# Earlier loads for three phases, and keys turned in place, in a one-core hybrid decoder step

## The reference, cut to what matters

```
logits = jnp.einsum('bqhe,bqkhe->bqhk', qg, kg) * SCALE
p, lse = masked_softmax(logits + bias[None], valid[None, :, None, :])
o = jnp.einsum('bqhk,bqkhe->bqhe', p.astype(vg.dtype), vg)
```

```
ha = jnp.einsum('bcjge,jef->bcgf', ch, w1[:CMP_STRIDE])
hb = jnp.einsum('bcjge,jef->bcgf', ch, w1[CMP_STRIDE:])
h = jax.nn.gelu(ha[:, :-1] + hb[:, 1:] + const)
```

## Time and profile before

| what | value |
|---|---|
| median of 3 runs | 2420.94 us (2412.12 to 2422.14) |
| the profiled execution | 2420.17 us, span 2418.3 us |
| mean granted TensorE clock | 0.914 |
| PE busy | 2060.2 us (85%) |
| DVE busy | 1248.5 us (52%) |
| ACT busy | 889.8 us (37%) |
| POOL busy | 141.9 us (6%) |
| DMA | 341.78 MB, mean 141 GB/s |

### The profile page before, as it was taken

The page is one execution under the profiler, slowest core; times in us unless marked ns, Lnnn a source line. Parts: engine busy times, 40 slices in busy tenths (PEclk is TensorE's granted clock), DMA queues, the critical chain, the costliest instruction groups (busy, mean ns, idle before and its releaser), DMA issues. The chain is left out here.

```text
span 2418.3 us, 40665 instructions
## 1 busy us (share of the span) xinstructions
PE 2060.2 (85%) x15344; PEld 1719.2 (71%) x15344; DVE 1248.5 (52%) x2596; ACT 889.8 (37%) x1482; POOL 141.9 (6%) x428
## 2 busy tenths in 40 slices
PE   7996567565987999999979679669997889999997
PEld 5993245443566999988779545446675779999786
DVE  4224456876754555544532468524444645555445
ACT  2211233234722544533221167523343234454432
POOL 3001000100000111100000000000000001111000
PEclk9997788787998999999989589879999889999999
DMA  5356288533132556642123331273331235665421
GB/s 164 127 189 203 80 315 288 206 150 121 50 122 95 194 201 217 205 146 74 61 95 84 107 94 47 75 215 146 119 131 39 93 117 200 218 203 191 140 82 49
DMA packets 169184, 341.78 MB, mean 141 GB/s; under 512 B 38175, under 2 KB 106319, under 8 KB 165051
## 3 DMA queue, kind: packets, MB, share of 16 engines
q1 hardware_dynamic: 152638, 200.40, 26.2%
q10 hardware_dynamic: 12956, 85.06, 10.5%
q0 software_dynamic: 3456, 54.53, 5.7%
HBM read 312.91 MB, written 97.35 MB: 170 GB/s over the span
## 5 line engine op out<-in xcount | busy, mean ns | idle before, releaser
L235 PE MATMUL ffn_acc<-x_h,ffn_wh 128*128 128x288 f32 x1408 | 303.5, 297 | 11.3 <-DVE ffn_wl L227 11.3
L235 PE MATMUL ffn_acc<-x_l,ffn_wh 128*128 128x288 f32 x1408 | 303.0, 297 | 0.0
L235 PE MATMUL ffn_acc<-x_h,ffn_wl 128*128 128x288 f32 x1408 | 302.8, 297 | 0.0
L235 PEld LDWEIGHTS ffn_acc<-x_h,ffn_wh 128*128 128x128 f32 x1408 | 228.2, 190 | 11.8 <-DVE ffn_wl L227 11.7
L235 PEld LDWEIGHTS ffn_acc<-x_l,ffn_wh 128*128 128x128 f32 x1408 | 228.3, 190 | 0.0
L235 PEld LDWEIGHTS ffn_acc<-x_h,ffn_wl 128*128 128x128 f32 x1408 | 228.3, 190 | 0.0
L227 DVE TENSOR_TENSOR ffn_wl<-ring,ffn_wh 128x2048 fp32r<-128x2048 f32 (+1 forms) x88 | 154.3, 1756 | 74.4 <-ACT ffn_wh L1980 74.4
L1936 PE MATMUL ffn_acc<-ffn_wh,x_h 128*128 128x512 f32 x440 | 175.5, 399 | 10.4 <-DVE ffn_wl L227 10.4
L1937 PE MATMUL ffn_acc<-ffn_wl,x_h 128*128 128x512 f32 x440 | 173.1, 393 | 0.0
L1938 PE MATMUL ffn_acc<-ffn_wh,x_l 128*128 128x512 f32 x440 | 172.9, 393 | 0.0
L227 DVE TENSOR_TENSOR x_l<-ffn_hid,x_h 128x1152 fp32r<-128x1152 f32 x44 | 59.7, 1358 | 153.8 <-ACT x_h L2037 153.8
(11 more groups left out here) (410 smaller groups left out, 4216.8 us busy)
## 6 DMA issues: line engine op xcount, KB each, us to landing
out_s_b_kv<-state_b_kv ACTq DMA_DIRECT2D x80, 768.0 KB, 7.8
ring<-ffn_up SPq DMA_DIRECT2D x44, 1024.0 KB, 6.7
ring<-ffn_down SPq DMA_DIRECT2D x44, 512.0 KB, 3.4
sb_k<-state_b_kv SPq DMA_DIRECT2D x8, 2048.0 KB, 13.1
sb_v<-state_b_kv SPq DMA_DIRECT2D x8, 2048.0 KB
proj_ab_w<-w_in_ab SPq DMA_DIRECT2D x11, 1024.0 KB, 5.5
ring<-w_in_c SPq DMA_DIRECT2D x7, 1024.0 KB, 5.3
hT_ab<-proj_ab_stage ACTq DMA_DIRECT2D x22, 288.0 KB, 2.1
```

Source lines behind the costliest of these rows:

```text
L235: done = pe.matmul(o, weights, x, start=start, stop=stop)
```

## The change

1. **Inputs of `sb`.** Keys of batch 0, queries, new keys and the 16 table rows are issued on SP at the start of `pidx` (`SampleBInputs`), and POOL clears `nat` there.
2. **Loop of `sb`.** ACT copies turned keys back over the loaded ones (`k[b % 3]`, three buffers), and `kT` with L1467 is gone; four small matmuls score the new keys from `k_new`. The keys of batch b+3 are asked for when batch b+1 is scored. Values of batch b-1 come after the first three tiles of the keys of b+1, and turn_out of b-1 after all of them. ACT makes the `pT` copies. DVE does 3 rounds ahead of the loop, then 4, 4, 4, 4, 4, 5, 4, 0; scaling and mixing run one batch late.
3. **Between `sb` and `sa`.** Both first gathers of `sa` go out when batch 6 is scored, into two key buffers of `sb`. `cross` stands at the end of `sb`'s SP, `merge` in `sb`'s last batch, the mask's memset on POOL. In `sa` keys are turned in place too, and the mask stands ahead of the table.
4. **`pc` and `sc`.** SP issues the 8 `phi_w1` DMAs in `pc`, ahead of its fourth query block, and POOL issues gathers 0 and 1 of `sc` there once the first pair is scored. The tables of `sc` land in the memory of `pT` and `pwT`. ACT makes the copies of the hidden values.

The rest of the diff is places of memory.

```diff
 def prompt_indexer_phase
+        def _(pool):
+            ahead.clear(pool)
         def _(sp):
+            ahead.load(sp)
 def prompt_attention_phase
+                if m == 3 and ahead is not None:
+                    ahead.load(sp)
                 if m >= 3:
                     sp.wait_ge(logit_ready, 2 * per_pair * (m - 2))
...
+                pool.wait_ge(logit_ready, 2 * per_pair)
+                for c in range(2):
+                    ahead.gather(pool, c)
 def sample_a_phase
-            for b in range(1, NB):
+            for b in range(2, NB):
...
-            choice.cross(sp)
             selection.load(sp)
...
-                    act.copy(kT[:, m % 2, s, i * 512:(i + 1) * 512], tps[f % 2][:, :]).then_inc(emptied, 1)
-                if b == 0:
-                    act.wait_ge(loaded, 48)
-                act.copy(kT[:, m % 2, s, PAST:LS], k_new[:, b * NS:(b + 1) * NS]).then_inc(kT_new, 1)
+                    act.copy(turned_keys((2 * m + s) % 4, i), tps[f % 2][:, :].rearrange("p (j c) -> p j c", j=4)).then_inc(emptied, 1)
...
+            choice.mask(dve, shifted[:, 0:SC])
             dve.wait_ge(t_in, 16 * 2 * NS)
...
-            steps = choice.merge(dve, shifted[:, 0:lists], shifted[:, lists:2 * lists], merged)
-            choice.mask(dve, sel_mask, shifted[:, 0:SC], merged, steps, masked)
 def sample_b_phase
-        k = p.sb("k", [P, 2, NT_K, 512])
-        kT = p.sb("kT", [P, 4, L])
+        k = [pre.k0, p.sb("k1", [P, NT_K, 512]), k2]
+        head_rounds, rounds = 3, (4, 4, 4, 4, 4, 5, 4, 0)
...
-                if r == 6 * selection.ROUNDS // NB:
-                    pool.wait_ge(out_ready, 5)
-                    sa_in.gather(pool, cache_a_kv, keep)
+                if r == selection.ROUNDS - rounds[NB - 2]:
+                    pool.wait_ge(logit_ready, NB - 1)
+                    sa_in.gather(pool, 0, k[0], cache_a_kv, keep)
+                    sa_in.gather(pool, 1, k[2], cache_a_kv, keep)
...
+            for b in range(2):
+                pre.rows(sp, k[b + 1], b + 1, 0, k_in[b + 1])
+                values_of(b)
             for b in range(NB):
-                if b >= 2:
-                    sp.wait_ge(turned_k, NT_K * (b - 1))
-                load(sp, k, b, 0, k_in[b % 2])
+                if b + 3 < NB:
+                    sp.wait_ge(logit_ready, b + 1)
+                    pre.rows(sp, k[b % 3], b + 3, 0, k_in[b % 3])
+                if 1 <= b < NB - 1:
+                    sp.wait_ge(out_ready, b)
+                    values_of(b + 1)
             sp.wait_ge(tabled, 4)
             sa_in.load(sp, hT, vec, new_a_kv)
+            selection.cross(sp)
...
-                    act.copy(kT[:, :, t * P:(t + 1) * P], tps[n % 2][:, :].rearrange("p (m c) -> p m c", m=4)).then_inc(kT_ready, 1)
-                act.copy(kT[:, :, NT_K * P:L], k_new[:, :, b * NS:(b + 1) * NS]).then_inc(kT_new, 1)
+                    act.copy(k[b % 3][:, t, :], tps[n % 2][:, :]).then_inc(kT_ready, 1)
...
+                if b == NB - 1:
+                    lists = selection.ROUNDS * 8
+                    selection.merge(dve, table[:, 0:lists], table[:, lists:2 * lists])
                 if b:
-                    dve.wait_ge(o_turned, b)
...
+                    mix_in(b - 1)
+            scale(NB - 1)
+            mix_in(NB - 1)
 def sample_c_phase
-            gather(0)
-            pool.wait_ge(tabled, 4)
-            gather(1)
...
-                    sp.dma_start(w1[g * HD:(g + 1) * HD, a, :, ab * HD:(ab + 1) * HD], src).then_inc(w1_in, 16)
...
+                    for a in range(2):
+                        for g in range(2):
+                            act.copy(hid[:, a, g, :], h_bank(c, g)[HD:P, a * P + 1:(a + 1) * P]).then_inc(h_moved, 1)
...
-                    dve.tensor_copy(hid[:, a, g, :], ps[HD:P, 1:NCH]).then_inc(h_moved, 1)
```

More of the change, by code:

```diff
@@ L557, in prompt_indexer_phase @@
         block = p.body.enter_context(nc.Block())
+        @block.gpsimd
+        def _(pool):
+            ahead.clear(pool)
         @block.sync
         def _(sp):
+            ahead.load(sp)
             for i in range(1, NQ):
@@ L665, in _ @@
                                                             ap=[[1, P], [LU, 2], [1, SEQ + P]])).then_inc(t_in[m % 3], 16)
+        if ahead is not None:
+            @block.gpsimd
+            def _(pool):
+                pool.wait_ge(logit_ready, 2 * per_pair)
+                for c in range(2):
+                    ahead.gather(pool, c)
         @block.tensor
@@ L884, in mask @@
         dve.wait_ge(step, n + 4)
+        dve.wait_ge(masked, 1)
         for h in range(2):
@@ L1442, in turn_out @@
                 pe.wait_ge(scaled, b + 1)
+                pe.wait_ge(pT_ready, min(2 * b + 4, 2 * NB))
                 pe.transpose(tpp[:, 11, :], o[:, :], keep.ident[:, :]).then_inc(o_turned, 1)
-            keys(0)
+            keys(0, 0, NT_K)
             for b in range(NB):
                 scores(b)
+                if b + 1 < NB:
+                    keys(b + 1, 0, 3)
+                if b:
+                    values(b - 1)
+                if b + 1 < NB:
+                    keys(b + 1, 3, 5)
+                turn(b)
+                if b + 1 < NB:
+                    keys(b + 1, 5, NT_K)
                 if b:
                     turn_out(b - 1)
-                if b + 1 < NB:
-                    keys(b + 1)
-                turn(b)
-                values(b)
+            values(NB - 1)
             turn_out(NB - 1)
@@ L1505, in mix_in, with scale, select @@
                     dve.tensor_copy(keep.mixT[r, 4:8, SEQ + b * NS:SEQ + (b + 1) * NS], src).then_inc(mixed, 1)
+            def scale(b):
+                dve.wait_ge(probs_ready, b + 1)
+                dve.reciprocal(rinv[:, b % 2:b % 2 + 1], total[:, b % 2:b % 2 + 1]).then_inc(weighed, 1)
+                dve.wait_ge(weighed, b + 1)
+                dve.wait_ge(out_ready, b + 1)
+                if b:
+                    dve.wait_ge(o_turned, b)
+                dve.tensor_scalar(o[:, :], outp, rinv[:, b % 2:b % 2 + 1], None, ALU.mult).then_inc(scaled, 1)
+            done = 0
+            def select(n):
+                for r in range(done, done + n):
+                    selection.round(dve, r)
+                return done + n
+            done = select(head_rounds)
             for b in range(NB):
@@ L2342, in _, with __init__, gather, load @@
             weigh(NQ - 1)
-def sample_c_phase(nc, hT, vec, cache_kv, state, new_kv, new_win, io, keep):
-    rows_in_cache = cache_kv.rearrange("n (c j) s g e -> (n c) (j s g e)", j=STRIDE)
+class SampleCInputs:
+    def __init__(self, nc, ctx, cache_kv, phi_w1, keep):
+        self.kv = ctx.enter_context(nc.sbuf_tensor("sc_kv", [P, 2, STRIDE * 512], F32))
+        self.w1 = ctx.enter_context(nc.sbuf_tensor("sc_w1", [P, 2, STRIDE, P], F32))
+        self.rows = cache_kv.rearrange("n (c j) s g e -> (n c) (j s g e)", j=STRIDE)
+        self.phi_w1, self.keep = phi_w1, keep
+    def gather(self, pool, c):
+        pool.indirect_dma_start(out=self.kv[:, c % 2, :], out_offset=None, in_=self.rows,
+                                in_offset=bass.IndirectOffsetOnAxis(ap=self.keep.chunk_row[:, c:c + 1], axis=0)).then_inc(self.keep.c_kv_in[c % 2], 16)
+    def load(self, sp):
+        for a in range(2):
+            for ab in range(2):
+                for g in range(2):
+                    src = self.phi_w1[a, 16 * ab:16 * (ab + 1)].rearrange("j e f -> e j f")
+                    sp.dma_start(self.w1[g * HD:(g + 1) * HD, a, :, ab * HD:(ab + 1) * HD], src).then_inc(self.keep.c_w1_in, 16)
+def sample_c_phase(nc, hT, vec, pre, state, new_kv, new_win, io, keep):
     R = N_HEADS * NS
@@ L2736, in _ @@
                     act.copy(kT[:, PAST:LS], k_new[:, 0, c * NS:(c + 1) * NS]).then_inc(kT_new, 1)
+                    act.wait_ge(h_done, 8 * c + 8)
+                    if c:
+                        act.wait_ge(kc_done, c)
+                    for a in range(2):
+                        for g in range(2):
+                            act.copy(hid[:, a, g, :], h_bank(c, g)[HD:P, a * P + 1:(a + 1) * P]).then_inc(h_moved, 1)
                     for a in range(2):
@@ L3011, in build @@
             ] + [(io["o_s_c_win"][b, C_WIN - NS:C_WIN, :], tok[b * NS:(b + 1) * NS, NQ, 512:768]) for b in range(NB)], io, keep)
+            compressed.close()
+            sc_in = SampleCInputs(nc, early, io["cache_c_kv"], io["phi_w1"], keep)
             prompt_attention_phase(nc, "pc", [
```

267 lines of the change are left out of this document (135 added, 132 removed).

## The result

The changed kernel takes 2338.28 us (median of 4 runs, 2335.95 to 2343.41) beside 2418.73 for the kernel before (4 runs, 2412.12 to 2422.14); the ratio is 0.9673, 95% interval 0.9646 to 0.9701. The profiled execution took 2343.41 us with a span of 2341.5, 76.8 us under the span before; the sum had said 77. (By the medians the kernel is 80 us shorter.)

A forecast was written before the change was run, and what follows sets the result against it. The chain of waits, no single engine, bounds `sb`'s loop; `sc`'s loop is PE-bound. Terms -44 (`sb`), -8 (seam), -20 (head of `sc`) and -5 (its loop) sum to -77, taking 2420.2 to 2343 us; range 2324 to 2378.

The forecast's parts named there:

- Earlier inputs of `sb`: Head of `sb`: with its keys already there, PE reaches first scores at 295.5, 10.8 us earlier.
- The loop: Loop of `sb`: a batch takes 15.3 us instead of 18.46, bounds 13.8 and 17.
- The floor of the DMA engines: Loop of `sb`: moving 5.32 MB a batch at 387 GB/s takes at least 13.7 us.
- The tail: From scores of batch 7 to the end of `sb`: taken as unchanged, 18.9 us.
- rival C: End of `sb`: two gathers collide with the last values, which land some 8 us late; 2351 us, chance 0.12.
- The seam: Between `sb` and `sa`: table and merge leave DVE's path to the mask, -8 us, bounds -8 and 0.
- `pc`: Eight weight DMAs ahead of query block 3 on SP may jam there: nothing, up to +5 us.
- The head of `sc`: Start of `sc`: weights and two gathers already there, gates without a jam, -20 us, bounds -9 and -28.
- rival B: Head of `sc`: gates jam all the same, 18.58 us instead of 7.4; 2354 us, chance 0.12.
- The loop of `sc`: Loop of `sc`: DVE loses its copies, so PE waits less for its `pT`; -5 us, between 0 and -7.5.
- Rival A: Loop of `sb`: keeps its 18.46 us period as one late load stalls the softmax; 2367 us, chance 0.15.
- Rival D: Loop of `sc`: PE idles a little and loses its clock, so slower, 2535 us at 0.50; chance 0.03.

## Why the prediction was right, and where it was not

- *Earlier inputs of `sb`* (-10.8): right, -11.2; undone alone, 13.5 us at the mask.
- *The loop* (15.3 us a batch, bounds 13.8 and 17): too long. The six distances are 14.0 on average, just inside the bounds; the steady one, 13.2, is below the lower one. The step that failed is "PE: 13.48 + 0.2 = 13.7 us, at the mean clock of 0.89". That clock was no given: it belonged to a PE that idled 27% of the time. With the waits gone the granted clock is 1.00 and the same work takes 11.7; with the old order, at a clock of 0.91 (352.78 to 370.91), it takes 13.1 again. The floor of the DMA engines, 13.7, was no floor either: at 384 GB/s a batch of 13.26 us moves 5.1 MB of the 5.32 that were reckoned, and with fewer values to load the batch is no shorter. That loads made ahead cover the difference is likely and was not tested. And "each holds up another now and then" was true above all for the batch of five rounds: 17.1 us, a row of numbers in the change that the prediction passed over.
- *The tail* ("I take what it is now, 18.9 us"): wrong, 30.4. The exchange was named as standing at the end of SP's queue, and what it was moved past, 19 loads and a collision, was not counted. From the scores of batch 7 to the end of `sb` it is 22.0 us with the exchange first (392.40 to 414.42) and 14.7 with late gathers besides (393.32 to 407.97). So the tail of before was no measure either; what stretched it is the exchange's place and rival C, whose condition held (PE waited 3.84 us for the last values). In the changed kernel C did not end the phase by the values, as the rival had it, but by the exchange.
- These two errors, -9.3 at the scores of batch 7 and +11.5 behind them, cancel; the sum for `sb` was off by 2.4 us only for that reason, which is luck.
- *The seam* (-8): right, -8.6, though no run undoes it alone. *`pc`* (0): right; its matmuls of scores start from 1404.1 to 1545.3 before and from 1355.0 to 1496.3 after, 141.2 and 141.3 us.
- *The head of `sc`* (-20, of which 2.1 for the second sequence's gather): right in its mechanism and 6 us too small. The first compressed keys come 20.5 us earlier in the phase (17.9 were reckoned to that point), with the gates at 7.76 us against the forecast 7.4: rival B did not come. The second sequence gains 5.6 us: its compressed keys stood 38.1 us behind the first ones, in the row of before below, and stand 32.5 behind them now (1539.44 to 1571.94). Of that 2.1 is the wait for the gather; 2.6 is PE's own work, 33.6 us at a granted clock of 0.89 before and 31.0 at 0.95 now, so this term went wrong as the loop of `sb` did.

```profile
1647.16 0.43 PE L2527 MATMUL sc_cps<-sc_hid,sc_w 64*64 64x127 f32 x4
```

- *The loop of `sc`* (-5): the six distances behind that gain 4.1 us together (32.76 each before, 32.0 to 32.4 now), and the run with the copies on DVE shows 3.9 to hang on them.
- That the total is right to a microsecond is luck as well: against the sum, `sb` is 2.4 us worse, `pc` 1, the loop of `sc` 1 and what stands behind its eighth sequence 2.5, where nothing was to change, and the head of `sc` is 6 better.
- Rival A did not come. The loop has a period near the old one with the old order (18.1 us) or with `pT` on DVE (17.2), but not by A's mechanism, a late load that stalls ACT. Rival D did not come: the loop of `sc` stands at a clock of 1.00 and PE is busy 98% of it.
- One bound was added up wrongly: 295.5 + 13.4 + 6 x 17 + 18.9 + 5.4 is 435.2 and not 430.4, so that all worst bounds together give -32 and not -37. The result lies far from both.

## What to carry to other kernels

Where an engine's wait is taken away, price its work at the clock that it gets when it is kept busy, not at the clock of the stretch with the waits. Where an instruction moves to the end of a queue, count what is issued ahead of it and who waits for it: two small DMAs behind 19 others cost 8 us here, more than the merge that they feed takes (414.51 to 419.94). And an engine's share of busy time says little about whether a job may be moved to it; what counts is what will stand behind the job in that engine's order.
